# A transformer block's first stage: transposed x features on a second DMA queue, both value halves first, norm factor at eviction, memory features loaded transposed

## Chip, core and metric

One NeuronCore of a Trainium2 chip runs the whole program in one launch. The metric is the device time of one execution in microseconds (us); lower is better. TensorE is PE (its weight loads PEld), VectorE DVE, ScalarE ACT, GpSimd POOL, SyncE SP.

## The reference

A block of 256 positions with 1024 features: RMS norm and one input projection, spatial gating, forgetting attention, output projection, SwiGLU; then a second block with pooling, mLSTM, grouped attention, cross-attention to a memory of 256 rows and 16 experts. What the change touches:

```python
h = rmsnorm(x, mix_pre_g[l])
proj = h @ w_in[l]
u, v_s, q, k, v_a, g_a, g_b, f_logit = jnp.split(proj, IN_SPLITS, axis=-1)
...
merged = jax.nn.sigmoid(g_a) * y_a + jax.nn.sigmoid(g_b) * y_b
x = x + rmsnorm(merged @ w_out[l], mix_post_g[l])
...
kv = (mem @ wkv).reshape(b, mem.shape[1], 2, CA_HEADS, CA_HEAD_DIM)
```

Here `rmsnorm` is x * rsqrt(mean(x*x) + 1e-6) * g per position, `v_a` are the attention values, and `mem` is used without a norm.

## The kernel before

**Split weights.** A float32 matrix product is made of three products of float32r operands: high x low, low x high, high x high (`mm3`, lines 357 to 360; `wide`, lines 378 and 379, packs two of them into one matmul of 512 columns). So every operand is split into a high part, written by ACT, and a low part (value minus high), written by DVE. The dense weights arrive in 85 units of 1 MB, each in four pieces of 128x512. SP loads unit u into one of three buffers RAW (line 2300), waiting for the low parts of unit u-3. ACT's `high` (line 1048) and DVE's `low` (line 1575) write a piece into one of five pairs SPH and SPL. The constant `POOL_PIECES` gives some low parts to POOL instead (line 2194). Pieces are taken in strict order by number, unit 4u+q.

**Order of work.** Nothing is scheduled: each engine's program is written out by hand and runs in order, and engines wait on each other's counters. A wait or a DMA issue holds all that stands behind it on its engine.

**The start.** x arrives in three DMAs, position rows on partitions. ACT and DVE square it, POOL takes the power -0.5 (`power`, line 2185), DVE multiplies by that factor and by the gain (`first_norm`, line 1616; PE had spread the gain row over all partitions, line 418), PE transposes the result through PSUM (`turn_tile`, line 409), ACT and DVE write its high and low parts XTH and XTL (lines 1058 and 1580). Only then can the first product run: `rtile` (lines 389 to 400) for the first 512 value columns (units 0 and 1), tile t being 128 of the 256 positions. The second tile is transposed between (line 425). Then q and k of heads 0 to 3 (`wide`, units 2 to 5), the second 512 value columns (units 6 and 7, lines 466 to 470), q and k of heads 4 to 7, and so on. ACT copies finished values from PSUM to VA (`values_out`, line 1099). After its first sixteen weight pieces ACT issues nine DMAs for constants (lines 1085 to 1093).

**The output projection.** After the product for u (lines 517 to 523), PE transposes the memory rows (line 532, 16 transposes through all four PSUM banks), then runs `out_tile` (lines 535 to 545). It uses units 28 to 31, pieces 112 to 127; POOL writes the low parts of pieces 120 to 123. ACT and DVE then write the memory's high and low parts MEMH and MEML (lines 1208 and 1767), which `wblock` needs later (line 557).

**The end.** From about 500 us on SP fills the expert buffers RING (400 MB of expert weights), each fill waiting for an event of the dense part, and then streams all 16 experts.

Of the kernel before, what the change touches and what calls it, by code (L numbers as in the profile page):

```python
# [13 lines left out]
P = 128  # L14
T = 256
# [11 lines left out]
U_VA, U_Q, U_K = (0, 6), (2, 8), (4, 10)  # L27
# [6 lines left out]
POOL_PIECES = (120, 121, 122, 123, 279, 283, 287, 293, 294, 295, 298, 299, 302, 303, 306, 307, 310, 311, 322, 327, 331, 335)  # L34
# [53 lines left out]
def build(nc, ctx, io, out):  # L88
# [25 lines left out]
    PIOTA = place("PIOTA", [P, 4], F32, SMALL + 128)  # L114
    ONER = place("ONER", [16, P], F32R, low(14))
# [8 lines left out]

    QT = place("QT", [P, 8, T], F32, at(135))
# [21 lines left out]
    MEM = place("MEM", [P, 2, D], F32, at(185))  # L147
# [86 lines left out]
    GROW = place("GROW", [1, D], F32, at(201))  # L234
# [70 lines left out]
    rn = {n: small() for n in ss}  # L305
    fox_small = [[small(2) for _ in range(3)] for _ in range(8)]
# [40 lines left out]
    def tensor(e):  # L347
# [66 lines left out]
        for _ in range(7):  # L414
            e.matmul(PB[4][:, 0:P], WARM[:, :], WARM[:, :], start=True, stop=True)
        e.wait_ge(s_row, 16)
        for i in range(2):
            e.matmul(PB[6 + i][:, :], WARM[0:1, :], GROW[:, halves[i]], start=True, stop=True).then_inc(*mixd.up(("gain", i)))  # L418
        for _ in range(2):
            e.matmul(PB[4][:, 0:P], WARM[:, :], WARM[:, :], start=True, stop=True)  # L420
        e.wait_ge(s_id, 16)
# [8 lines left out]
        free = {0: vec.at(("xt_in", 1, 0)), 1: vec.at(("xt_in", 1, 1)), 2: act.at(("va", 0, 0)), 3: act.at(("va", 0, 1))}  # L430
# [63 lines left out]
        for h in range(2):  # L494
            for t in range(2):
                bank = 2 - 2 * h + t
                e.wait_ge(*free[bank])
                rtile(U_VS + 2 * h, bank, t, [("xt_in", t, j) for j in range(2)], ("vs", h, t))
                free[bank] = act.at(("vs", t, h))
# [26 lines left out]
        e.wait_ge(s_mem, 16)  # L526
        for t in range(2):
            for j in range(2):
                b = 2 * t + j
                e.wait_ge(*free[b])  # L530
                for k in range(4 * j, 4 * j + 4):
                    i = e.transpose(PB[b][:, (k % 4) * P:(k % 4 + 1) * P], MEM[:, t, k * P:(k + 1) * P], ident)
                i.then_inc(*turn.up(("mem", t, j)))

# [497 lines left out]
    def scalar(e):  # L1032
        done = [0]

        def high(n):

            for _ in range(n):
# [35 lines left out]
        e.dma_start(X[:, 0, 512:1024], io["x"][0:P, 512:1024]).then_inc(s_x[1], 16)  # L1073
        e.dma_start(GROW[:, :], io["mix_pre_g"].rearrange("(a n) -> a n", a=1)).then_inc(s_row, 16)
        squares_in(0, 0, "x0", (s_x[0], 16))
        high(2)
        for j in range(2):
            high_turned(0, j, j, XTH, turn.at(("in", 0, j)), "xt_in")
        high(2)
        pre_squares(1, "x1", [(s_x[2], 16)] * 2)  # L1080
        high(4)
        for j in range(2):
            high_turned(1, j, j, XTH, turn.at(("in", 1, j)), "xt_in")
        high(8)
# [60 lines left out]

        for half_ in range(2):
            for t in range(2):
                values_out(half_, t)
# [10 lines left out]
            if half_ == 0:  # L1159
                high(8)  # L1160
# [1388 lines left out]
```

## Time and profile before

| | |
|---|---|
| median of 3 runs | 1486.63 us (1486.63 to 1488.58) |
| the profiled execution | 1486.36 us, of which span 1484.6 us |
| PE busy | 1147.1 us (77%) |
| DVE, ACT, POOL busy | 468.4, 398.3, 74.1 us |
| DMA | 503.33 MB, mean 339 GB/s |

The profile is one execution. Its 40 slices show PE at nine tenths in the first 14 and at five to six tenths after; the DMA engines are at nine tenths from about the 16th on. The two stretches have to be read apart: in each it is asked what PE waits for.

### The profile page before, as it was taken

How to read it: one execution, taken by the hardware profiler on the slowest of the kernel's cores; microseconds unless marked ns; L12 is line 12 of the kernel's file. 1: busy time of each engine (PE TensorE's matmuls, PEld its weight loads, DVE VectorE, ACT ScalarE, POOL GpSimd, SP SyncE). 2: the span in 40 equal slices, each digit the busy share in tenths (PEclk: the TensorE clock that was granted, in tenths of full speed). 3: DMA queues.
4: the chain of work that ended last, by engine and by line, in shares of the span. 5: the costliest groups of instructions: out<-in, count | busy, mean ns of one | idle time of the engine just before them, and what ended most of it. 6: DMA issues, size and time to landing. Idle time of an engine off the chain costs nothing.

```text
span 1484.6 us, 19383 instructions
## 1 busy us (share of the span) xinstructions
PE 1147.1 (77%) x8336; PEld 754.3 (51%) x8336; DVE 468.4 (32%) x954; ACT 398.3 (27%) x890; POOL 74.1 (5%) x89
## 2 busy tenths in 40 slices
PE   9999999999999998995566466566665564565677
PEld 7888988888877875442322223223222232232234
DVE  6575777656788764110000000000000000000002
ACT  5665567555657642110000000000000000000002
POOL 0000020000035411000000000000000000000000
PEclk9999999999999998798778778787887787887789
DMA  8435546555553488999999999999999999999996
GB/s 313 171 138 203 198 172 223 208 207 199 199 187 114 149 347 343 397 436 434 433 437 426 433 433 435 424 442 430 430 437 426 438 430 433 433 426 440 423 424 288
DMA packets 29450, 503.33 MB, mean 339 GB/s; under 512 B 4275, under 2 KB 4915, under 8 KB 8245
## 3 DMA queue, kind: packets, MB, share of 16 engines
q1 hardware_dynamic: 25344, 493.43, 79.7%
q10 hardware_dynamic: 4020, 8.66, 1.6%
q8 instruction: 66, 1.08, 0.3%
q14 instruction: 20, 0.16, 0.0%
HBM read 501.03 MB, written 1.05 MB: 338 GB/s over the span
## 4 chain that ended last, share of the span: by engine, by line
issue 60%; PE 32%; DVE 5%; ACT 1%; POOL 1%; POOLq 0%; DVEq 0%; ACTq 0%
PE PB L378 9%; PE PB L358 5%; PE PB L359 5%; PE PB L360 5%; PE PB L379 4%; DVE SPL L1575 1%; DVE XN L1595 0%; PE PB L409 0%; POOL SP L2238 0%; PE PB L815 0%; PE PB L680 0%; PE PB L418 0%; PE PB L507 0%; PE PB L799 0%; PE PB L454 0%
## 5 line engine op out<-in xcount | busy, mean ns | idle before, releaser
L919 PE MATMUL PB<-RING,XS 128*32 128x512 f32 x2048 | 292.8, 720 | 177.0 <-DMA RING<-in_wgu_dram 176.7
L919 PEld LDWEIGHTS PB<-RING,XS 128*32 128x32 f32 x2048 | 68.4, 126 | 345.3 <-issue 249.8
L951 PE MATMUL PB<-RING,HHT 128*32 128x256 f32 x2048 | 150.9, 452 | 111.9 <-DMA RING<-in_wdn_dram 110.5
L1575 DVE TENSOR_TENSOR SPL<-RAW,SPH 128x512 fp32r<-128x512 f32 x318 | 207.0, 709 | 31.4 <-ACT SPH L1048 28.7
L378 PE MATMUL PB<-XT,SPH 128*128 128x512 f32 x544 | 194.1, 401 | 0.0
L1048 ACT ACTIVATE SPH<-RAW 128x512 fp32r<-128x512 f32 x340 | 186.8, 620 | 7.4 <-DMA RAW<-in_wst_dram 3.3
L951 PEld LDWEIGHTS PB<-RING,HHT 128*32 128x32 f32 x2048 | 75.3, 129 | 172.2 <-issue 141.7
L379 PE MATMUL PB<-XT,SPL 128*128 128x256 f32 x544 | 152.4, 280 | 0.0
L1506 ACT ACTIVATE SG<-PB 128x512 f32<-128x512 f32 x16 | 9.6, 597 | 506.1 <-PE PB L919 506.1
L2128 DVE SCALAR_TENSOR_TENSOR YL<-PB,COLS,YH 128x256 fp32r<-128x256 f32 x64 | 31.0, 484 | 279.0 <-ACT YH L1520 279.0
L378 PEld LDWEIGHTS PB<-XT,SPH 128*128 128x128 f32 x544 | 102.2, 188 | 24.6
L379 PEld LDWEIGHTS PB<-XT,SPL 128*128 128x128 f32 x544 | 102.7, 189 | 0.4
L1520 ACT ACTIVATE YH<-PB,COLS 128x256 fp32r<-128x256 f32 x64 | 30.3, 474 | 252.7 <-PE PB L951 252.7
L2118 DVE TENSOR_TENSOR SG<-SG,PB 128x512 f32<-128x512 f32 x16 | 11.0, 687 | 268.2 <-ACT SG L1506 268.2
L2113 DVE TENSOR_TENSOR XS<-PB,RG 128x256 f32<-128x256 f32 x15 | 6.4, 425 | 234.7 <-PE PB L905 234.7
L2185 POOL TENSOR_TENSOR SM<-SM,MH 128x1 f32<-128x1 f32 (+3 forms) x20 | 15.2, 762 | 1287.0 <-DVE SM L2170 886.7
L905 PEld LDWEIGHTS PB<-SEL,X 128*128 128x128 f32 x480 | 54.7, 192 | 12.1 <-issue 11.7
L905 PE MATMUL PB<-SEL,X 128*128 128x32 f32 x480 | 56.4, 277 | 0.3 <-DVE COLS L2132 0.3
L970 PEld LDWEIGHTS PB<-YL,GT 128*128 128x128 f32 x128 | 25.7, 201 | 41.8 <-issue 39.0
L358 PE MATMUL PB<-SPH,XT 128*128 128x512 f32 x112 | 44.9, 401 | 1.7 <-DVE XT L1580 1.7
L358 PE MATMUL PB<-XT,SPL 128*128 128x256 f32 x160 | 46.0, 287 | 0.0
L360 PE MATMUL PB<-XT,SPH 128*128 128x256 f32 x160 | 45.3, 283 | 0.0
(398 smaller groups left out, 1577.5 us busy)
## 6 DMA issues: line engine op xcount, KB each, us to landing
RAW<-in_wst_dram SPq DMA_DIRECT2D x84, 1024.0 KB, 4.9
RING<-in_wgu_dram SPq DMA_DIRECT2D x13, 2048.0 KB, 40.4
RING<-in_wgu_dram SPq DMA_DIRECT2D x4, 4096.0 KB, 22.3
RING<-in_wgu_dram SPq DMA_DIRECT2D x14, 1024.0 KB, 8.1
RING<-in_wdn_dram SPq DMA_DIRECT2D x6, 2048.0 KB, 13.4
RING<-in_wdn_dram SPq DMA_DIRECT2D x2, 4096.0 KB, 19.0
RING<-in_wdn_dram SPq DMA_DIRECT2D x3, 1024.0 KB, 41.0
RAW<-in_wst_dram SPq DMA_DIRECT2D x4, 256.0 KB, 5.6
```

The costliest lines, as they stand in the source:

```text
L358: e.matmul(out_, ll, rh, start=first, stop=False)
L359: e.matmul(out_, lh, rl, start=False, stop=False)
L360: return e.matmul(out_, lh, rh, start=False, stop=final)
L378: e.matmul(both, hv[:, k, c], XT[:, :, k, :], start=k == 0, stop=False)
L379: i = e.matmul(PB[bank][:, 0:T], lv[:, k, c], XTH[:, k, :], start=False, stop=k == KD - 1)
L905: i = e.matmul(PB[3][:, 32 * k:32 * k + 32], X[:, t, k * P:(k + 1) * P], SEL[:, t, 32 * x:32 * x + 32], start=t == 0, stop=t == 1)
L919: i = e.matmul(PB[b][32 * c:32 * c + 32, :], XS[x % 2][:, k, :], chunk_at(n)[:, 512 * c:512 * c + 512], start=k == 0, stop=k == KD - 1)
L951: w = e.matmul(PB[b][32 * j:32 * j + 32, 0:T], HHT[:, j, 32 * c:32 * c + 32], chunk_at(n)[:, T * (4 * (c % 2) + j):T * (4 * (c % 2) + j + ...
L1048: e.activation(h, src, ACT.Copy).then_inc(*hi.up())
L1520: e.activation(YH[m % 2][:, :], PB[3 - m % 2][:, 0:T], ACT.Copy, scale=COLS[:, 1, x:x + 1]).then_inc(*act.up(("y", x, m)))
L1575: e.tensor_tensor(l, src, h.bitcast(F32), ALU.subtract).then_inc(*lo.up())
L2128: e.scalar_tensor_tensor(out=YL[m % 2][:, :], in0=PB[3 - m % 2][:, 0:T], scalar=COLS[:, 1, x:x + 1], in1=YH[m % 2][:, :].bitcast(F32), op0 ...
```

## The change

- **x.** A transposed copy `xt` (feature on the partition, host layout) comes in four DMAs of 256 KB on ACT's queue, behind the gain as a column (`GCOL`, 4 KB). x itself, now needed only for the squares and the residual, moves on SP's queue behind the first three weight units. The ACT table is loaded by a small activation first. The identity moves from SP's to ACT's queue.
- **Rows without the norm factor.** For the first four feature blocks of tile 0 ACT and DVE multiply by the gain column and split in one step each (`high_first`, `low_first`). The other three quarters POOL multiplies by the gain (128x512 each), then ACT and DVE split them (`high_rows`, `low_rows`) into XRH and XRL. The fourth POOL multiply is for the first quarter itself.
- **Values first.** Units 0 to 3 are now the two value halves; each piece is used for both tiles. The norm factor is ACT's scale when it copies values out. PE's two products `norm_factors` (inside the second half) spread the factors over the partitions, DVE multiplies all of XR by them, ACT and DVE split that into XTH and XTL for all other projections. ACT's nine constant DMAs stand behind this split, and the two value evictions of half 0, the eight pieces of units 4 and 5, and the evictions of half 1 behind those.
- **Removed on PE.** 16 transposes and two gain products of the start, 16 transposes of the memory; 13 warming products in place of 7 + 2.
- **Memory.** It is loaded transposed; ACT and DVE split it from SBUF.
- **Pieces 120 to 123** move from POOL to DVE.

```diff
-U_VA, U_Q, U_K = (0, 6), (2, 8), (4, 10)
+U_VA, U_Q, U_K = (0, 2), (4, 8), (6, 10)
...
-POOL_PIECES = (120, 121, 122, 123, 279, 283,
+POOL_PIECES = (279, 283,
...
 def tensor(e):
...
-        rtile(U_VA[0], 2, 0, [("xt_in", 0, j) for j in range(2)], ("va", 0, 0), between=second_tile)
-        rtile(U_VA[0], 3, 1, [("xt_in", 1, j) for j in range(2)], ("va", 0, 1))
+        for half_ in range(2):
+            for j in range(2):
+                first_pairs = [(0, 0), (1, 0), (0, 1), (1, 1)]
+                for k, t in (first_pairs if half_ + j == 0 else [(k, t) for k in range(2) for t in range(2)]) + [(k, t) for k in (2, 3) for t in range(2)]:
...
+                    i = rk(U_VA[half_] + j, k, 4 * j + k, 2 - 2 * half_ + t, XRH, XRL, t, j + k == 0, j == 1 and k == 3)
...
+                    if (half_, j, k, t) == (1, 0, 1, 1):
+                        norm_factors()
+        free = {b: act.at(("va", int(b < 2), b % 2)) for b in range(4)}
...
-                for k in range(4 * j, 4 * j + 4):
-                    i = e.transpose(PB[b][:, (k % 4) * P:(k % 4 + 1) * P], MEM[:, t, k * P:(k + 1) * P], ident)
...
 def scalar(e):
+        e.dma_start(GCOL[:, :], io["mix_pre_g"]).then_inc(s_gcol, 16)
+        for j in range(2):
+            for t in range(2):
+                e.dma_start(XR[:, t, 4 * j:4 * j + 4, :], io["xt"][:, t, 4 * j:4 * j + 4, :]).then_inc(s_xt[2 * j + t], 16)
...
+        high_first(0)
+        high(1)
+        for k in range(1, 4):
+            high_first(k)
+        high(1)
+        high_rows(1, 0)
+        high(2)
+        high_rows(0, 1)
+        high_rows(1, 1)
+        high(4)
...
-            e.activation(VA[:, t, halves[half_]], PB[bank][:, :], ACT.Copy).then_inc(*act.up(("va", half_, t)))
+            e.activation(VA[:, t, halves[half_]], PB[bank][:, :], ACT.Copy, scale=rn[f"x{t}"]).then_inc(*act.up(("va", half_, t)))
...
+        for t in range(2):
+            values_out(0, t)
+        high(8)
+        for t in range(2):
+            values_out(1, t)
...
 def vector(e):
+            scaled_rows = XR[:, :, 4 * j:4 * j + 4, :].rearrange("p t k c -> p k t c")
+            factors = PB[6][:, 0:T].rearrange("p (t c) -> p t c", t=2).unsqueeze(1).to_broadcast([P, 4, 2, P])
+            e.tensor_tensor(scaled_rows, scaled_rows, factors, ALU.mult).then_inc(*vec.up(("n_in", j)))
...
 def gpsimd(e):
+        for t, j in ((1, 0), (0, 1), (1, 1), (0, 0)):
...
+            a = XR[:, t, 4 * j:4 * j + 4, :]
+            e.tensor_tensor(a, a, GCOL[:, 4 * j:4 * j + 4].unsqueeze(2).to_broadcast([P, 4, P]), ALU.mult).then_inc(*gps.up(("xg", t, j)))
...
-        low(120, 121, 122, 123)
...
 def sync(e):
+        for i in range(2):
+            c = slice(1024 * i, 1024 * i + 1024)
+            e.dma_start(RAW[1][:, c], io["wst"][1][:, c]).then_inc(s_next[i], 16)
+        e.dma_start(RAW[2][:, :], io["wst"][2]).then_inc(s_w[2], 16)
+        for t in range(2):
+            e.dma_start(X[:, t, :], io["x"][t * P:(t + 1) * P, :]).then_inc(s_x[t], 16)
```

**Place one: ACT, from the end of the first sixteen weight pieces to the values' evictions** (SPH is a piece's high part, the number its buffer; XT the normed input; VA the values; PB a PSUM bank). Before:

```order
L1048 ACTIVATE SPH3<-RAW0 128x512 [waits s_w0]
L1048 ACTIVATE SPH3<-RAW0 128x512 x3
L1085 DMA WFR<-in_wf_dram 128x1024
...
L1093 DMA PIOTA<-in_piota_dram 128x4
L1099 ACTIVATE VA<-PB2 128x512 [waits s_product]
L1099 ACTIVATE VA<-PB3 128x512 [waits s_product]
L1048 ACTIVATE SPH4<-RAW1 128x512 [waits s_w1]
```

Now:

```order
L1051 ACTIVATE SPH3<-RAW0 128x512 x3
L1109 ACTIVATE XT<-XR 128x1024 [waits s_formed] x2
L1111 DMA WFR<-in_wf_dram 128x1024
...
L1119 DMA PIOTA<-in_piota_dram 128x4
L1125 ACTIVATE VA<-PB2,SM 128x512 [waits s_product,s_pooled]
L1125 ACTIVATE VA<-PB3,SM 128x512 [waits s_product]
L1051 ACTIVATE SPH4<-RAW1 128x512 [waits s_w1]
L1051 ACTIVATE SPH4<-RAW1 128x512 x3
L1051 ACTIVATE SPH0<-RAW2 128x512 [waits s_product,s_w2]
L1051 ACTIVATE SPH0<-RAW2 128x512 x3
L1125 ACTIVATE VA<-PB0,SM 128x512 [waits s_product]
```

The split of the normed input, which waits for DVE (`s_formed`), now stands ahead of the nine DMAs, and the eviction that frees bank 0 behind eight more weight pieces. PE's first product of q writes bank 0.

**Place two: DVE, the start** (SPL is a piece's low part; XRL that of a row quarter). Before:

```order
L1616 SCALAR_TENSOR_TENSOR XN<-X,SM,PB6 128x512 [waits s_mixed,s_pooled]
L1616 SCALAR_TENSOR_TENSOR XN<-X,SM,PB7 128x512 [waits s_mixed]
L1575 TENSOR_TENSOR SPL0<-RAW0,SPH0 128x512 [waits s_high] x2
L1580 TENSOR_TENSOR XT<-PB0,XT 128x4x128 [waits s_activated]
L1580 TENSOR_TENSOR XT<-PB1,XT 128x4x128 [waits s_activated]
```

Now:

```order
L1649 SCALAR_TENSOR_TENSOR XRL<-XR,GCOL,XRH 128x128 [waits s_activated,s_xt0,s_gcol]
L1604 TENSOR_TENSOR SPL0<-RAW0,SPH0 128x512 [waits s_high]
L1649 SCALAR_TENSOR_TENSOR XRL<-XR,GCOL,XRH 128x128 [waits s_activated] x3
L1604 TENSOR_TENSOR SPL0<-RAW0,SPH0 128x512 [waits s_high]
L1641 TENSOR_TENSOR XRL<-XR,XRH 128x4x128 [waits s_activated]
L1604 TENSOR_TENSOR SPL0<-RAW0,SPH0 128x512 [waits s_high] x2
L1641 TENSOR_TENSOR XRL<-XR,XRH 128x4x128 [waits s_activated] x2
```

PE's second product (feature block 1, tile 0) waits for the second weight piece, behind three short rows; its first product for tile 1 waits for the first L1641. Each of the rows of now reads two operands from SBUF; of those of before L1580 and L1616 read one from PSUM.

**Place three: POOL, the start.** Before:

```order
L2196 MEMSET WARM 128x128
L2197 MEMSET MH 128x16
L2198 MEMSET ONER 16x128
L2185 ISA
L2185 TENSOR_TENSOR SM<-SM,MH 128x1 [waits s_formed,s_pooled]
```

Now, behind the same memsets:

```order
L2251 TENSOR_TENSOR XR<-XR,GCOL 128x512 [waits s_xt1,s_gcol]
L2251 TENSOR_TENSOR XR<-XR,GCOL 128x512 [waits s_xt2]
L2251 TENSOR_TENSOR XR<-XR,GCOL 128x512 [waits s_xt3]
L2251 TENSOR_TENSOR XR<-XR,GCOL 128x512 [waits s_xt0,s_formed]
L2230 TENSOR_TENSOR SM<-SM,MH 128x1 [waits s_formed,s_pooled]
```

The four multiplies by the gain stand ahead of the powers that give the norm factor; the fourth waits for DVE's short rows.

## Rows read from the trace of the kernel before

**Rows 1.** Busy time by stretch: each engine's us, granted clock, DMA share, GB/s.

```profile
40.00:200.00 160.00, 159.96 (x1022) 145.13 (x1022) 107.77 (x250) 97.23 (x220) 5.84 (x6) 1.00 0.47 173
600.00:1484.00 884.00, 565.87 (x5006) 259.73 (x4998) 60.43 (x131) 56.47 (x114) 0.82 (x1) 0.81 0.99 425
```

**Rows 2.** Timeline of PE at the start: start, us, instruction, idle before.

```profile
8.06 1.22 PE L420 MATMUL PB<-WARM 128*128 128x128 f32 x4
11.54 0.79 PE L358 MATMUL PB<-SPH,XT 128*128 128x512 f32 x1 [0.56 <-DVE XT L1580]
12.99 0.63 PE L358 MATMUL PB<-SPH,XT 128*128 128x512 f32 x1
13.42 0.63 PE L359 MATMUL PB<-SPL,XT 128*128 128x512 f32 x1
15.52 0.40 PE L358 MATMUL PB<-SPH,XT 128*128 128x512 f32 x1
25.07 0.39 PE L360 MATMUL PB<-SPH,XT 128*128 128x512 f32 x1
25.30 0.39 PE L378 MATMUL PB<-XT,SPH 128*128 128x512 f32 x1
```

**Rows 3.** DMA issues to 30 us: count, KB each, median us to landing.

```profile
RAW<-in_wst_dram SPq DMA_DIRECT2D x4, 256.0 KB, 5.6
X<-in_x_dram ACTq DMA_DIRECT2D x1, 256.0 KB, 3.4
```

**Rows 4.** The first six us, columns as in rows 1.

```profile
0.00:6.00 6.00, 4.94 (x16) 3.89 (x17) 0.86 (x3) 2.00 (x3) 1.14 (x8) 1.00 0.62 182
```

**Rows 5.** Timelines of POOL, of DVE beside it, and of DVE alone.

```profile
195.79 5.96 POOL L2194 TENSOR_TENSOR SPL<-RAW,SPH 128x512 fp32r<-128x512 f32 x4 [46.75 <-ACT SPH L1048]
198.81 1.78 DVE L1575 TENSOR_TENSOR SPL<-RAW,SPH 128x512 fp32r<-128x512 f32 x1
19.67 4.89 DVE L1575 TENSOR_TENSOR SPL<-RAW,SPH 128x512 fp32r<-128x512 f32 x8
```

**Rows 6.** POOL's and DVE's lines, durations ns min/median/max, then DVE and POOL groups.

```profile
L2194 POOL TENSOR_TENSOR SPL<-RAW,SPH x22: 1270/1594/1879, 195.8 to 537.9; 128x512 fp32r<-128x512 f32 x22
L2253 POOL TENSOR_TENSOR RWG<-RW,RG 128x128 f32<-128x128 f32 x1 | 0.9, 932 | 0.0
L1602 DVE TENSOR_TENSOR XN<-PB,G 128x512 f32<-128x512 f32 x8 | 5.2, 683 | 2.5 <-ACT JUNK L1067 2.5
L1786 DVE TENSOR_TENSOR FL<-FL,PB 128x256 f32<-128x256 f32 x22 | 9.3, 421 | 24.7 <-ACT FL L1240 24.7
```

**Rows 7.** Timeline of ACT and its issue queue (ACTq) before the first eviction; eight pieces elsewhere.

```profile
18.76 0.36 ACTq L1085 DMA_DIRECT2D WFR<-in_wf_dram  x1
22.82 0.48 ACTq L1093 DMA_DIRECT2D PIOTA<-in_piota_dram  x1
23.35 0.60 ACT L1099 ACTIVATE VA<-PB 128x512 f32<-128x512 f32 x1 [1.25 <-PE PB L360]
209.93 4.26 ACT L1048 ACTIVATE SPH<-RAW 128x512 fp32r<-128x512 f32 x8
```

**Rows 8.** PE after a wait in the expert stage, and that stretch by the us.

```profile
811.52 1.08 PE L919 MATMUL PB<-RING,XS 128*32 128x512 f32 x4 [5.32 <-DMA RING<-in_wgu_dram]
813.00:814.00 1.00, 1.00 (x8) 0.20 (x4) 0.00 (x0) 0.00 (x0) 0.00 (x0) 0.50 0.60 262
815.00:816.00 1.00, 1.00 (x16) 0.36 (x12) 0.00 (x0) 0.00 (x0) 0.00 (x0) 1.00 1.51 655
```

**Rows 9.** Timeline of PE, ACT and DVE around the memory's transposes.

```profile
192.60 2.17 PE L532 MATMUL PB<-CON,MEM 128*128 128x128 f32 x16
194.52 0.47 PE L358 MATMUL PB<-SPH,MTL 128*128 128x512 f32 x1
195.10 1.14 ACT L1048 ACTIVATE SPH<-RAW 128x512 fp32r<-128x512 f32 x2
195.22 0.42 DVE L1741 TENSOR_TENSOR MTL<-QT,MTH 128x256 fp32r<-128x256 f32 x1 [0.48 <-ACT MTH L1191]
```

More of the change, by code:

```diff
@@ L267, in build @@
     s_first = [sem(f"s_first{q}") for q in range(4)]
+    s_next = [sem(f"s_next{i}") for i in range(2)]
     s_w = [sem(f"s_w{i}") for i in range(NRAW)]
@@ L413, in tensor @@
         e.wait_ge(*gps.at("warm"))
-        for _ in range(7):
+        for _ in range(13):
             e.matmul(PB[4][:, 0:P], WARM[:, :], WARM[:, :], start=True, stop=True)
[L416 to L421, printed above, removed]
@@ L497, in tensor @@
                 e.wait_ge(*free[bank])
-                rtile(U_VS + 2 * h, bank, t, [("xt_in", t, j) for j in range(2)], ("vs", h, t))
+                rtile(U_VS + 2 * h, bank, t, [("xt_in", j) for j in range(2)], ("vs", h, t))
                 free[bank] = act.at(("vs", t, h))
@@ L1205, in scalar @@
         e.wait_ge(*vec.at(("gu", 7)))
-        for t in range(2):
-            for j in range(2):
-                high_turned(t, j, 2 * t + j, MEMH, turn.at(("mem", t, j)), "memt")
+        e.wait_ge(s_mem, 16)
+        for q in range(4):
+            e.activation(MEMH[:, 2 * q:2 * q + 2, :], MEM[:, 2 * q:2 * q + 2, :], ACT.Copy).then_inc(*act.up(("memt", q)))
         post_squares(0, "po0", "out")
@@ L1607, in postnorm @@
                 e.scalar_tensor_tensor(out=X[:, t, c], in0=XN[:, t, c], scalar=rn[name], in1=X[:, t, c], op0=ALU.mult, op1=ALU.add).then_inc(*vec.up((out_name, t, h)))
-        def first_norm(t, name):
-            e.wait_ge(*gps.at(("r", name)))
-            for h in range(2):
-                c = halves[h]
-                if t == 0:
-                    e.wait_ge(*mixd.at(("gain", h)))
-                e.scalar_tensor_tensor(out=XN[:, t, c], in0=X[:, t, c], scalar=rn[name], in1=PB[6 + h][:, :], op0=ALU.mult, op1=ALU.mult).then_inc(*vec.up(("n_in", t, h)))
@@ new lines, in vector, with low_first @@
+        e.wait_ge(s_gcol, 16)
+        e.wait_ge(s_xt[0], 16)
+        def low_first(k):
+            e.wait_ge(*act.at(("xr0", k)))
+            e.scalar_tensor_tensor(out=XRL[:, k, 0:P], in0=XR[:, 0, k, :], scalar=GCOL[:, k:k + 1], in1=XRH[:, k, 0:P].bitcast(F32),
+                                   op0=ALU.mult, op1=ALU.subtract).then_inc(*vec.up(("xr0", k)))
+        low_first(0)
+        low(1)
+        for k in range(1, 4):
+            low_first(k)
+        low(1)
+        low_rows(1, 0)
@@ new lines, in vector @@
+        low(2)
+        low_rows(0, 1)
+        low_rows(1, 1)
+        low(8)
+        for t in range(2):
+            e.wait_ge(s_x[t], 16)
+            e.tensor_tensor_reduce(XN[:, t, halves[1]], X[:, t, halves[1]], X[:, t, halves[1]], 1.0 / D, 0.0, ALU.mult, ALU.add, ss[f"x{t}"][1]).then_inc(*vec.up())
+        for t in range(2):
+            mean_square(f"x{t}", act.at((f"x{t}", 0)), vec.so_far())
+        low(4)
+        e.wait_ge(*gps.at(("xg", 0, 0)))
+        e.wait_ge(*mixd.at("r_in"))
@@ L1764, in vector @@
         low(8)
-        for t in range(2):
-            for j in range(2):
-                low_turned(t, j, 2 * t + j, MEMH, MEML, "memt")
+        for q in range(4):
+            e.wait_ge(*act.at(("memt", q)))
+            e.tensor_tensor(MEML[:, 2 * q:2 * q + 2, :], MEM[:, 2 * q:2 * q + 2, :], MEMH[:, 2 * q:2 * q + 2, :].bitcast(F32), ALU.subtract).then_inc(*vec.up(("memt", q)))
         postnorm(0, "po0", 1, 16, "res_mix")
```

130 lines of the change are left out of this document (69 added, 61 removed).

## The prediction

> **What bounds the kernel now.** I read the busy times by stretch first. From 40 to 200 us PE is busy for 159.96 of 160 us, and in the expert stage the DMA engines are at 0.99 of their time with 425 GB/s while PE waits [rows 1]. So the dense part ends when PE's list is done, and the expert stage, gated by events of the dense part, moves with it: a us gained or lost on PE at the start or around 195 us is a us of the whole time, and work on ACT, DVE or POOL counts only where PE waits for it. Second I read PE's timeline of the start. The first product starts at 11.54; its matmuls come 0.43 us apart (12.99, 13.42) until 15.52, and 0.23 apart later (25.07, 25.30); q starts at 25.30 [rows 2]. The granted clock reads 1.00 there too [rows 4], but 512 columns in 0.43 us are 1.2 GHz, and in 0.23 nearly 2.4. What stands before 11.54 is what the change attacks.
>
> **The yardstick.** The change puts both value halves ahead of q. Before, only one half lies ahead; the other's 48 matmuls come later, 48 x 0.228 = 10.9 us. So q of the changed kernel starts even with before at 25.3 + 10.9 = 36.2. Earlier is gain, later is loss, us for us.
>
> **Part 1: when the rows are there.** The first transposed quarter is second on ACT's queue, issued at about 1.3; an x half of the same size landed 3.4 us after its issue [rows 3], so it is there at about 4.7, and the first piece's split makes a first product possible at about 6.3. The second piece and the second quarter need four transfers, 1.05 MB, to have landed. In its first 6 us the kernel moved 6 x 182 = 1.09 MB [rows 4], so 6.1. Bound from above: the four first weight quarters took a median of 5.6 us to land [rows 3], 1 to 1.5 us later than this.
>
> **Part 2: POOL's multiplies hold DVE.** POOL has four new multiplies of 128x512. A POOL operation of that size takes 1.27 us at least [rows 6]. DVE's own pieces take 4.89 / 8 = 0.61 us apart alone, but one started at 198.81, while POOL did four, took 1.78 [rows 5], that is 0.68 and nearly a whole POOL operation. So I take turns: each multiply holds DVE for 1.27 us, then DVE does one row. DVE's short rows are an estimate: 0.68 at 512 and 0.42 at 256 columns [rows 6] give 0.29 at 128. From 6.2: three turns of 1.27 + 0.29 end at 10.9, the second piece is split at 11.5, the fourth multiply and the first rows of tile 1 end at 13.4. Only from there does PE run without gaps. By the Trainium skill, page SBUF — State Buffer, section Who interferes with whom, a tensor_tensor with two SBUF inputs and a GpSimd instruction that reads SBUF exclude each other for the whole instruction, which speaks against this placement; the 1.78 agrees, and by that rule the whole change costs the 4.3 us below. Read as mere slowing (DVE at 0.68/1.78 of its pace beside POOL), 4 x 1.27 = 5.1 us of POOL would cost DVE 3.1 instead of 5.1, and everything below would be 2 us less: +2.3. I take the turns, because four pieces beside POOL show the wait before an operation, not a longer one. Bounds: nothing (POOL ready while DVE is idle anyway), and 4 x 0.93 = 3.7 us for each multiply, if a broadcast multiply goes by the element like the 128x128 one [rows 6].
>
> **Part 3: to the norm factors.** PE's products for the factors stand behind 20 of 32 triples of matmuls. Two triples are done by 13.4, for tile 0 alone. The array stands at the lower level: before, it needed 11.54 to 15.52, 3.98 us, for three triples [rows 2]. So 13.4 + 4.0 + 15 x 3 x 0.228 = 27.6, and 28.0 with the two small products. DVE is not later: 14 pieces and two rows at 0.61, squares and small ones 1.8, from 13.4, is 25.0. X itself lands behind 3 MB of weights, and the powers follow DVE's squares at about 23; neither ends last.
>
> **Part 4: the queue on ACT.** Behind the factors: DVE multiplies twice 128x1024, an estimate by the same line as above 1.2 each, to 30.4. ACT's split waits for that, and in ACT's queue follow nine DMA issues. They cost 18.76 to 23.30, 4.5 us, and they hold ACT: its first eviction came at 23.35 after 1.25 us idle, put down to PE, which had long been done [rows 7]. Before, eight weight pieces queued ahead of them covered most of it; now nothing does. Then two evictions (1.1), eight pieces (4.26 [rows 7]), one eviction (0.6), which frees the bank of the first q product: 30.4 + 4.5 + 1.1 + 4.3 + 0.6 = 40.9. PE's values end at 28.0 + 36 x 0.228 = 36.2. So PE waits 4.7 us and q starts 4.7 us later than the 36.2 of before. The pieces of units 4 and 5 that q needs are behind the same queue and come 0.6 to 4 us earlier than the bank.
>
> **Part 5: the clock.** After a wait of 5.32 us the granted clock was 0.50 (1.2 GHz) from 813 to 814 and 1.00 (2.4 GHz) from 815 on: with the resumption at 811.5, some 3 us at half [rows 8]. I take the same for a wait of 4.7: 1.5 us of work. Bounds: nothing, and half of the 3.98 us at the lower level of the start [rows 2], 2.0.
>
> **Part 6: memory and output projection.** The 16 transposes go: 192.60 to 194.52, 1.9 us of PE [rows 9]. What covers: the first product needs no transpose; its eighth block needs the low part ending at 195.64, and comes at 192.6 + 7 x 0.68 = 197.4. Piece 120, now on DVE, is high at about 195.7 and low at 196.4 [rows 9], needed at 192.6 + 8 x 0.68 = 198.1; the next seven follow every 0.61 and are needed every 0.68. If DVE were 2 us late with them, the whole gain would be lost. ACT and DVE do the same number of splits for the memory as before.
>
> Nothing else: evictions with a scale are ACT rows as before; the start's 16 transposes and gain products lie inside parts 1 to 3; SP's fifth load waits for the same low parts.
>
> **Sum.** +4.7 + 1.5 - 1.9 = +4.3 us on the profiled execution's 1486.36, so **1490.7**. (The median of the runs is 0.3 above that execution.) What a measurement can tell from no change is 0.2%, 3 us.
>
> **Rivals.**
> - *POOL costs DVE little* (chance 0.25). Then the gap-free run starts at about 8.7, the factors are done at 8.7 + 4.0 + 10.2 + 0.4 = 23.3, q starts at 36.2, and the sum is 1.5 - 1.9: 1486.0. For it: before 6 us DVE has little, and multiplies that fit its waits are free. Against: 1.78 [rows 5].
> - *PE at the upper level from the start, and POOL mild: faster* (0.12). 13 warming products in place of 7. By the Trainium skill, page TensorE: Matmul & The Clock Gate, Part 1, sustained activity lifts the array's clock; in this trace the dummies did not: after them (8.06) the first real matmuls were still 0.43 apart [rows 2]. If it holds, 8.7 + 18 x 0.683 + 0.4 = 21.4 for the factors, q 1.8 before the yardstick, 1484.2; without the later fall of the clock 1482.7. It decides in favour when the factors' products are done before 23.7, 4.3 us ahead of my 28.0.
> - *POOL's broadcast multiplies are slow* (0.08): at 2 us each about 3 more, 1494; at 3.7, 1500.
>
> **Numbers.** Forecast 0.55, with 1488.7 to 1493 of its own. The range 1484 to 1495 leaves out most of the fast and slow rivals. Slower by over 0.2% (above 1489.6): 0.45 of the forecast, the slow rival and a little of the first, 0.55. Within 0.2%: 0.10 of the forecast and most of the first rival, 0.31. Faster: 0.14.
>
> **What would show it.** After: PE gap-free from about 13; POOL's four multiplies between 6 and 13 with DVE rows over 1 us long beside them; the factors' products near 28; ACT's nine issues from about 30 to 35 with ACT idle; a PE wait of 4 to 5 us ending near 41, with ACT's third eviction just before it, then matmuls at 0.43 us spacing. Wrong if that wait is absent, if DVE's early rows stay at 0.68, or if the output projection waits for pieces 120 to 127.

## The result, and the profile after

The changed kernel takes 1490.04 us (median of 13 runs, 1489.21 to 1492.61), the kernel before in the same measurement 1486.69 us (13 runs, 1484.79 to 1488.96). The ratio is 1.0026, its 95% interval 1.0019 to 1.0033: slower by 3.4 us. The profiled execution took 1490.07 us, 3.7 more than that of before. The forecast was 1490.7.

**A yardstick for the whole dense part.** Late in it PE waits for a normalised tile, in every kernel for the same 1 us. The start of the matmuls behind that wait is called M below. What happened earlier moves it, and what follows is the same program. Before, and after (timeline of PE: start, us, instruction, count, idle before and what ended it):

```profile
426.06 0.66 PE L409 MATMUL PB<-CON,XN 128*128 128x128 f32 x4 [1.02 <-DVE XN L1595]
```

```profile
430.31 0.66 PE L415 MATMUL PB<-CON,XN 128*128 128x128 f32 x4 [1.03 <-DVE XN L1624]
```

M went from 426.06 to 430.31, +4.25 us, beside a predicted sum of +4.3. From M to the end of the span it is 1058.54 us before and 1057.99 after; the 0.5 us between them is inside the scatter of that stretch (1057.1 to 1061.0 us over all profiles). From the first product of the output projection to M it is 231.5 us in every kernel but the one with pieces put back on POOL, so M follows the start us for us. The expert stage is what it was in [rows 1]:

```profile
600.00:1484.00 884.00, 575.10 (x5023) 262.96 (x5015) 60.58 (x132) 56.80 (x115) 0.81 (x1) 0.80 0.99 426
```

PE at the start, to be laid beside [rows 2]:

```profile
8.28 0.47 PE L364 MATMUL PB<-SPH,XRL 128*128 128x512 f32 x1 [2.53 <-DVE SPL L1604]
10.45 0.47 PE L364 MATMUL PB<-SPH,XRL 128*128 128x512 f32 x1 [1.24 <-DVE SPL L1604]
11.31 0.63 PE L364 MATMUL PB<-SPH,XRL 128*128 128x512 f32 x1
25.08 0.61 PE L428 MATMUL PB<-CON,SM 128*128 128x128 f32 x4
33.49 0.39 PE L366 MATMUL PB<-SPH,XRH 128*128 128x512 f32 x1
40.01 0.77 PE L384 MATMUL PB<-XT,SPH 128*128 128x512 f32 x1 [6.13 <-ACT VA L1125]
40.79 0.63 PE L384 MATMUL PB<-XT,SPH 128*128 128x512 f32 x1
45.26 0.39 PE L384 MATMUL PB<-XT,SPH 128*128 128x512 f32 x1
```

The first product comes 3.3 us earlier than before, but q starts at 40.01, 3.8 us behind the prediction's yardstick of 36.2, after a wait of 6.13 us for the eviction that frees its bank. The first eight steps of q then take 5.25 us (0.78 for the first, 0.64 for each of the others: 40.79, 41.43 and so on), and from 45.26 on a step takes 0.35. ACT in those microseconds, beside [rows 7]:

```profile
27.05 2.19 ACT L1109 ACTIVATE XT<-XR 128x1024 fp32r<-128x1024 f32 x2 [3.62 <-DVE XR L1673]
28.18 0.33 ACTq L1111 DMA_DIRECT2D WFR<-in_wf_dram  x1
33.19 0.45 ACTq L1119 DMA_DIRECT2D PIOTA<-in_piota_dram  x1
33.77 1.27 ACT L1125 ACTIVATE VA<-PB,SM 128x512 f32<-128x512 f32 x2 [4.53 <-PE PB L366]
34.92 4.26 ACT L1051 ACTIVATE SPH<-RAW 128x512 fp32r<-128x512 f32 x8
39.08 1.25 ACT L1125 ACTIVATE VA<-PB,SM 128x512 f32<-128x512 f32 x2
```

The nine issues run from 28.18 to 33.64. ACT is idle for 4.53 us, and the profile puts it down to PE, which had finished half 0 long before; that it waited for its own queue is what the first experiment tests. Behind that stand two evictions, eight pieces and the eviction that frees bank 0. The granted clock (columns as in [rows 1]; the seventh is the clock):

```profile
11.00:12.00 1.00, 1.00 (x4) 0.80 (x3) 1.00 (x1) 0.39 (x2) 0.84 (x1) 0.55 1.10 451
39.00:40.00 1.00, 0.00 (x0) 0.02 (x1) 1.00 (x1) 1.00 (x3) 0.64 (x1) 0.50 0.83 164
46.00:47.00 1.00, 1.00 (x7) 0.86 (x7) 0.91 (x2) 0.88 (x2) 0.00 (x0) 1.00 0.00 0
```

0.50 is the level of 1.2 GHz, 1.00 that of 2.4. It falls twice: at 11, after waits of 2.53 and 1.24 us (until 15), and during the wait for q. POOL and DVE at the start:

```profile
8.50 1.05 POOL L2251 TENSOR_TENSOR XR<-XR,GCOL 128x512 f32<-128x512 f32 x1 [7.32 <-DMA XR<-in_xt_dram]
12.74 2.59 POOL L2251 TENSOR_TENSOR XR<-XR,GCOL 128x512 f32<-128x512 f32 x2 [0.90 <-DMA XR<-in_xt_dram]
8.05 1.65 DVE L1649 SCALAR_TENSOR_TENSOR XRL<-XR,GCOL,XRH 128x128 fp32r<-128x128 f32 x3
12.91 2.97 DVE L1641 TENSOR_TENSOR XRL<-XR,XRH 128x512 fp32r<-128x512 f32 x2
```

POOL waited for its quarters, so its multiplies lie between 8.5 and 15.3, spread out; beside them two of DVE's rows are long (2.97 us together). At the memory, beside [rows 9], the last product of u is followed at once by the output projection:

```profile
198.72 0.28 PE L366 MATMUL PB<-XT,SPH 128*128 128x256 f32 x1
198.84 0.40 PE L364 MATMUL PB<-SPH,MTL 128*128 128x512 f32 x1
```

Read at three places the balance is: q +3.81 (40.01 for 36.2); at the end of u +6.24 (198.84 for 192.60), so 2.43 more from the half speed behind the wait; at the first product of the output projection +4.32 (198.84 for 194.52), so the transposes gave back 1.92.

### The profile page after: what moved, and what is told of

It reads as the page before. It is cut to its first block, busy times and chain, and to the rows that moved or that the text cites. A ratio compares the mean times of both kernels' runs of the same rounds, so it can differ in the third digit from the quotient of the medians.

```text
span 1488.3 us, 19356 instructions
## 1 busy us (share of the span) xinstructions
PE 1147.0 (77%) x8312; PEld 752.9 (51%) x8312; DVE 475.4 (32%) x963; ACT 401.0 (27%) x894; POOL 72.8 (5%) x89
## 3 DMA queue, kind: packets, MB, share of 16 engines
HBM read 502.08 MB, written 1.05 MB: 338 GB/s over the span
## 4 chain that ended last, share of the span: by engine, by line
issue 60%; PE 31%; DVE 5%; ACT 2%; ACTq 0%; DMA 0%; POOL 0%; POOLq 0%; DVEq 0%
PE PB L384 9%; PE PB L364 5%; PE PB L366 5%; PE PB L365 5%; PE PB L385 4%; DVE SPL L1604 1%; ACT SPH L1051 1%; DVE XN L1624 0%; DMA XR<-in_xt_dram 0%; PE PB L815 0%; PE PB L518 0%; ACT SP L1391 0%; PE PB L799 0%; PE PB L455 0%; PE PB L470 0%
## 5 line engine op out<-in xcount | busy, mean ns | idle before, releaser
L2230 POOL TENSOR_TENSOR SM<-SM,MH 128x1 f32<-128x1 f32 (+3 forms) x20 | 15.3, 765 | 1338.8 <-DVE SM L2215 886.3
L366 PE MATMUL PB<-XT,SPH 128*128 128x256 f32 x160 | 45.3, 283 | 0.0
L365 PE MATMUL PB<-XT,SPH 128*128 128x256 f32 x160 | 45.2, 283 | 0.0
## 6 DMA issues: line engine op xcount, KB each, us to landing
RING<-in_wdn_dram SPq DMA_DIRECT2D x6, 2048.0 KB, 13.4
```

The lines of the kernel that those rows point to most:

```text
L365: e.matmul(out_, lh, rl, start=False, stop=False)
L366: return e.matmul(out_, lh, rh, start=False, stop=final)
```

## The experiments

Each ran beside the kernel before on one chip, with five rounds of timing. The chips differ from set to set, but the kernel before took 1486.5 to 1486.8 us on all of them, so the medians can be laid side by side. **Theory A**: q is late by ACT's order, the nine issues and the bank; the clock's fall is a loss of its own; the memory part is a gain by itself. **Theory B**: q is late because POOL and DVE are slow at the start.

### Undoing ACT's order: issues, banks, both

The nine issues behind the evictions:

```diff
-        e.dma_start(WFR[:, :], io["wf"]).then_inc(s_wf, 16)
...
         for t in range(2):
             values_out(1, t)
+        e.dma_start(WFR[:, :], io["wf"]).then_inc(s_wf, 16)
...
```

> The changed kernel, with ACT's nine constant DMAs moved from behind the split of the normed input to behind the evictions of both value halves. Theory A (the nine issues hold ACT 5.5 us and with it the eviction that frees q's first bank): the two evictions of half 0 come at about 29.3 instead of 33.8, the eight pieces end at 34.7, q starts at about 35.4 instead of 40.0; the wait of PE shrinks from 6.1 to 1.5 us. That is 4.6 us, and 7.0 us if the clock then no longer falls (2.4 us at half speed). So 4.6 to 7.0 us under the changed kernel. Theory B (q waits for the normed input itself, that is for DVE and POOL at the start): q stays within 1 us of 40.0 and the time does not change.

Measured: 1485.18 us, ratio to before 0.9996 (0.9987 to 1.0004), 4.9 us under the changed kernel by the medians.

```profile
29.63 1.25 ACT L1116 ACTIVATE VA<-PB,SM 128x512 f32<-128x512 f32 x2
35.86 0.47 PE L384 MATMUL PB<-XT,SPH 128*128 128x512 f32 x1 [1.49 <-DVE SPL L1604]
```

The evictions came at 29.6, the wait shrank to 1.49, the clock stayed at 1.00 behind it, and M is 423.81, 6.5 less. Theory A, and in its numbers. B falls as the main cause.

The banks exchanged:

```diff
-                    i = rk(U_VA[half_] + j, k, 4 * j + k, 2 - 2 * half_ + t, XRH, XRL, t, j + k == 0, j == 1 and k == 3)
+                    i = rk(U_VA[half_] + j, k, 4 * j + k, 2 * half_ + t, XRH, XRL, t, j + k == 0, j == 1 and k == 3)
-        free = {b: act.at(("va", int(b < 2), b % 2)) for b in range(4)}
+        free = {b: act.at(("va", b // 2, b % 2)) for b in range(4)}
-            bank = t if half_ else 2 + t
+            bank = 2 * half_ + t
```

> The changed kernel, with the banks of the two value halves exchanged: half 0 writes banks 0 and 1, half 1 banks 2 and 3, so that q's first product needs the eviction of half 0 instead of that of half 1. The nine issues stay where they are. Theory A (bank 0 is what PE waits for): q then waits for the first piece of unit 4, which follows the two evictions at 33.8 to 34.9, high at 35.5 and low at 36.1: q at 36.1 instead of 40.0, a PE wait of 2.2 us; 3.9 us less, up to 6.3 if the clock does not fall. Theory B (normed input): no change.

Measured: 1486.64 us, 1.0004 (0.9995 to 1.0013), 3.4 under the changed kernel. The absolute times of the expectation missed, because in this execution the first quarter of x landed late: ACT waited 3.68 us for it.

```profile
8.61 0.40 ACT L1084 ACTIVATE XRH<-XR,GCOL 128x128 fp32r<-128x128 f32 x1 [3.68 <-DMA XR<-in_xt_dram]
11.10 0.76 PE L364 MATMUL PB<-SPH,XRL 128*128 128x512 f32 x1 [4.79 <-DVE SPL L1604]
39.73 0.47 PE L384 MATMUL PB<-XT,SPH 128*128 128x512 f32 x1 [1.81 <-DVE SPL L1604]
```

So the first product is 2.8 us later than in the changed kernel's profile and the last value product 4.0 (37.53 for 33.49), and still q starts 0.3 earlier, after a wait of 1.81 (2.2 expected) for the first piece and with no fall of the clock. M is 427.69, 2.6 less.

Both edits:

> Both edits of the two kernels beside this one: issues late and banks exchanged. Theory A: the first pieces of unit 4 are split at about 31 to 32, bank 0 is free at 30, the normed input's low parts end at 30.5, so PE goes from the last value product at 33.9 to q without a wait; 6.1 us of wait and 2.4 us of half speed go, 8.5 us under the changed kernel and some 5 under the kernel before. Theory B: no change. If the wait goes but the time falls by less than 7, the expert stage does not follow the dense part us for us.

Measured: 1484.16 us, 0.9984 (0.9974 to 0.9994): 2.4 under before, 5.9 under the changed kernel, less than the 8.5 expected.

```profile
34.38 0.39 PE L366 MATMUL PB<-SPH,XRH 128*128 128x512 f32 x1
34.61 0.39 PE L384 MATMUL PB<-XT,SPH 128*128 128x512 f32 x1
```

The wait is gone altogether. M is 422.49, 7.8 less, though the last value product came 0.9 later than in the changed kernel's profile (34.38 for 33.49): read at M, the 8.5 are there. That the medians show 5.9 may have two sources, neither tested by itself: landings differ from run to run, and from M to the end the span took 1057.1 to 1061.0 us over all profiles of this study, with no clear relation to M. So a difference of two medians is uncertain by a us and more, and M is the sharper reading.

### The memory part alone

The kernel before with the memory loaded transposed, its transposes removed and pieces 120 to 123 on DVE (the hunks of the change for `POOL_PIECES`, `MEM` and `memt`, and nothing else):

```diff
-POOL_PIECES = (120, 121, 122, 123, 279,
+POOL_PIECES = (279,
...
-                    i = e.transpose(PB[b][:, (k % 4) * P:(k % 4 + 1) * P], MEM[:, t, k * P:(k + 1) * P], ident)
...
+            e.activation(MEMH[:, 2 * q:2 * q + 2, :], MEM[:, 2 * q:2 * q + 2, :], ACT.Copy).then_inc(*act.up(("memt", q)))
```

> The kernel before with the last part of the change alone: memory loaded transposed, its 16 transposes removed, pieces 120 to 123 on DVE instead of POOL. Theory A: 1.9 us less than before, no PE wait in the output projection. Rival (the pieces or the memory's split come late on DVE, or the transposes only filled a wait for the first low part of the product's input): PE waits 0.6 to 2 us in the output projection and the time changes by less than 1 us.

Measured: 1484.61 us beside 1486.58, ratio 0.9990 (0.9980 to 0.9999), 2.0 us less.

```profile
26.03 0.39 PE L378 MATMUL PB<-XT,SPH 128*128 128x512 f32 x1
193.32 0.40 PE L358 MATMUL PB<-SPH,MTL 128*128 128x512 f32 x1
```

q began 0.73 us later than in [rows 2], the output projection 1.20 earlier than in [rows 9]: 1.93 in between, and PE waits nowhere in it. As expected. With that gain taken out, the rest of the change cost 4.25 + 1.92 = 6.2 us at M.

The pieces put back on POOL in the changed kernel:

```diff
-POOL_PIECES = (279,
+POOL_PIECES = (120, 121, 122, 123, 279,
...
+        low(120, 121, 122, 123)
```

> The changed kernel with the low parts of pieces 120 to 123 back on POOL. Theory A (DVE has time for them): no PE wait in the output projection with or without, and the time does not change (within 0.5 us); beside POOL some DVE rows last 1.8 us again. Rival (moving them to DVE gained or cost something): over 1 us either way, with a PE wait near 200 to 215 us.

Measured: 1494.28 us, 1.0045 (1.0031 to 1.0059), 4.2 over the changed kernel (2.7 over its control run below). Theory A missed here, and the rival holds:

```profile
203.23 5.93 POOL L2239 TENSOR_TENSOR SPL<-RAW,SPH 128x512 fp32r<-128x512 f32 x4 [46.74 <-ACT SPH L1051]
206.63 0.39 PE L366 MATMUL PB<-SPH,MTH 128*128 128x512 f32 x1
207.53 0.50 PE L364 MATMUL PB<-SPH,MTL 128*128 128x512 f32 x1 [0.50 <-POOL SPL L2239]
208.10 0.39 PE L366 MATMUL PB<-SPH,MTH 128*128 128x512 f32 x1
209.21 0.50 PE L364 MATMUL PB<-SPH,MTL 128*128 128x512 f32 x1 [0.73 <-POOL SPL L2239]
```

Without the transposes PE reaches pieces 120 to 123 sooner than POOL, at 1.48 us each, has them: two waits. The rows give them as 1.23 us of idle time, but read from start to start they cost 1.8: 0.90 from 206.63 to 207.53 and 1.11 from 208.10 to 209.21, and 0.33 and 0.34 from the first matmul behind each to the next, where matmuls otherwise come 0.23 apart. At M the kernel is 3.0 behind; q's own start, 41.22, is 1.2 of that, and the two waits are the rest.

### The clock, taken by itself

24 products of the warming tile between the last value product and q:

```diff
+        for _ in range(24):
+            e.matmul(PB[4][:, 0:P], WARM[:, :], WARM[:, :], start=True, stop=True)
+
         def fox_scores(h):
```

> The changed kernel with 24 matmuls of the warming tile on PE between the last value product and q, some 5.3 us of a wait of 6.1. Nothing that q waits for changes. Theory A (the fall of PE's clock after the wait is a loss of its own): q still starts near 40.0, but its matmuls come 0.34 us per pair at once instead of 0.64 up to 45.1; the time falls by 2.4 us. Rival (the clock falls there whatever PE does, or the loss is made up later): no change. Another rival (the matmuls hold up q): up to 1 us slower.

Measured: 1489.55 us, 1.0022 (1.0013 to 1.0031), only 0.5 under the changed kernel by medians.

```profile
36.38 5.52 PE L449 MATMUL PB<-WARM 128*128 128x128 f32 x48
41.80 0.50 PE L384 MATMUL PB<-XT,SPH 128*128 128x512 f32 x1
42.25 0.40 PE L384 MATMUL PB<-XT,SPH 128*128 128x512 f32 x1
```

q runs at 0.35 us a step at once. This execution started late (first product at 9.73), so q came 1.79 later than in the changed kernel, yet M is 429.78, 0.53 earlier: 2.3 us made up, next to 2.4 expected (next to the control run below it is 1.5, because there the clock cost less). The half speed is a loss of its own, shown at M, not in the medians.

More warming products at the start of the changed kernel:

```diff
-        for _ in range(13):
+        for _ in range(24):
             e.matmul(PB[4][:, 0:P], WARM[:, :], WARM[:, :], start=True, stop=True)
```

> The changed kernel with 24 warming products in place of 13, so that PE is busy until about 8.2 instead of 5.8. Theory A (the clock rises under the dummies and falls at 11 because PE then waited 2.5 us for its first and 1.2 us for its second product): the clock stays at the upper level, the matmuls from 11 to 14.6 come 0.23 instead of 0.43 us apart, the factors' products come 1.5 to 1.8 us earlier, and with them ACT's queue and q: 1.5 to 1.8 us less. Rival (the array must be busy with products for some us before the clock rises, dummies or not): no change, or 0.2 us slower.

Measured: 1491.09 us, 1.0028 (1.0016 to 1.0040): no gain.

```profile
1.06 8.56 PE L421 MATMUL PB<-WARM 128*128 128x128 f32 x48 [1.06 <-POOL MH L2242]
9.37 0.47 PE L364 MATMUL PB<-SPH,XRL 128*128 128x512 f32 x1
12.69 0.50 PE L364 MATMUL PB<-SPH,XRL 128*128 128x512 f32 x1 [1.69 <-DVE XRL L1641]
10.00:11.00 1.00, 1.00 (x5) 0.48 (x3) 0.00 (x0) 0.48 (x1) 0.48 (x1) 1.00 1.02 408
```

The mechanism is right and the forecast wrong: the clock stays at 1.00 all through the start, but 24 products last until 9.3 and held the first product up by a us, and then PE waits 1.69 us for rows that POOL and DVE have not made. A faster PE at the start finds nothing to do.

### POOL's multiplies

Left out, for the timing alone (the rows then lack the gain):

```diff
-        for t, j in ((1, 0), (0, 1), (1, 1), (0, 0)):
...
-            e.tensor_tensor(a, a, GCOL[:, 4 * j:4 * j + 4].unsqueeze(2).to_broadcast([P, 4, P]), ALU.mult).then_inc(*gps.up(("xg", t, j)))
```

> The changed kernel with POOL's four multiplies by the gain left out (so the gain is missing from all rows but the first four blocks of tile 0, and from the normed input). Theory of the prediction (POOL holds DVE for whole operations, and that delays PE): DVE's rows of 128x512 beside them fall from 1.0 to 1.5 us each to 0.6 to 0.7, the second product comes 0.6 us earlier, PE runs without gaps from about 9.9, the factors and q come 0.6 us earlier, 2.3 if the clock then does not fall at 11; 0.6 to 2.3 us less. Rival (DVE's delay is covered, because the quarters land late and PE runs at half speed anyway): DVE's rows shorten, the factors' products stay within 0.3 us, no change of the time.

Measured: 1490.28 us, 1.0018 (1.0009 to 1.0027), by medians no change.

```profile
8.21 0.87 DVE L1649 SCALAR_TENSOR_TENSOR XRL<-XR,GCOL,XRH 128x128 fp32r<-128x128 f32 x3
11.90 0.69 DVE L1641 TENSOR_TENSOR XRL<-XR,XRH 128x512 fp32r<-128x512 f32 x1
24.01 0.61 PE L428 MATMUL PB<-CON,SM 128*128 128x128 f32 x4
38.73 0.77 PE L384 MATMUL PB<-XT,SPH 128*128 128x512 f32 x1 [5.92 <-ACT VA L1125]
```

The three short rows take 0.87 us instead of 1.65, a row of 128x512 0.69 instead of 1.5. The factors come 1.07 earlier, q 1.28, M (428.44) 1.9. Next to the control below the factors come 2.4 earlier and q 1.9. So POOL cost one to two us at the start, and the wait for ACT stayed at 5.92. At q this lies inside the first expectation (0.6 to 2.3), while the median did not change, as the rival said; it is far from B.

Then rows split block by block with the gain as a scale, POOL's multiplies behind them, on top of late issues and exchanged banks:

```diff
+        def high_rows(t, j):
+            e.wait_ge(s_xt[2 * j + t], 16)
+            for k in range(4 * j, 4 * j + 4):
+                high_first(k, t)
...
+            e.wait_ge(*vec.at(("xr1", 7)))
             a = XR[:, t, 4 * j:4 * j + 4, :]
```

> The kernel with late issues and exchanged banks, and beside that the rows of all four quarters split as those of the first are, with the gain as a scale on ACT and DVE, block by block; POOL's four multiplies by the gain come behind the last of these rows. Theory (POOL holds DVE at the start, and what is late there is PE's second and third product): the short rows take 0.29 us each instead of 0.55, the second product comes 0.6 us earlier, the factors and q about 1 us earlier than with late issues and exchanged banks alone; 0.5 to 1.5 us less. Rival (ACT pays: 12 short rows of 0.32 us in place of three of 0.57, 2.2 us more on an engine that the weight pieces need too): nothing gained, or up to 1 us lost.

Measured: 1483.08 us, 0.9978 (0.9969 to 0.9987), 1.1 under both edits alone. The factors came at 25.19 instead of 25.97 and q at 34.19 instead of 34.61, less than half of what was expected at q:

```profile
14.58 5.92 POOL L2251 TENSOR_TENSOR XR<-XR,GCOL 128x512 f32<-128x512 f32 x4 [13.39 <-DVE XRL L1643]
14.57 8.29 DVE L1603 TENSOR_TENSOR SPL<-RAW,SPH 128x512 fp32r<-128x512 f32 x8 [0.17 <-ACT SPH L1049]
25.19 0.99 PE L428 MATMUL PB<-CON,SM 128*128 128x128 f32 x4 [1.05 <-POOL SM L2231]
```

The rest of the hold only moved. Four POOL operations stretched eight pieces from 4.9 us [rows 5] to 8.29, so DVE's squares, POOL's powers and the factors were late, and PE waited 1.05 us.

The same with `range(20)` warming products:

> The same with 20 warming products in place of 13: at 0.36 us each (24 took 8.56 us) they end at 8.2, just when the first product can start. Theory A (the clock stays at the upper level when PE has no wait of over a us): no half speed between 9 and 14, q 1 to 1.7 us earlier than without. Rival (pieces and rows come no faster, PE waits for them instead): q within 0.4 us, no change of the time.

Measured: 1483.42 us, 0.9976 (0.9967 to 0.9985). The clock stayed at 1.00, the third triple of products came at 10.30 instead of 11.12, and q at 34.13 instead of 34.19: the rival. The changed kernel itself once more:

> The changed kernel itself once more, beside the two above on the same chip. If its start varies with the landing of the first transfers from run to run, its first product will not be at 8.28 again but between 8.2 and 11.1, q between 40.0 and 42, the time 1489 to 1493; its ratio to before 1.002 to 1.004.

Measured: 1491.58 us, 1.0031 (1.0019 to 1.0042); first product 8.35, factors 26.43, q 40.63 after a wait of 5.40, M 430.09.

```profile
34.38 1.26 ACT L1125 ACTIVATE VA<-PB,SM 128x512 f32<-128x512 f32 x2 [3.80 <-issue]
40.63 0.77 PE L384 MATMUL PB<-XT,SPH 128*128 128x512 f32 x1 [5.40 <-ACT VA L1125]
43.96 0.39 PE L384 MATMUL PB<-XT,SPH 128*128 128x512 f32 x1
```

The first number of this start repeats, the next ones vary by up to 1.4 us. Two readings of the changed kernel's profile come out differently here. ACT's idle time is put down here to "issue", which means that ACT waited for nothing that the profile shows; so it is in five of the seven profiles with this order, and PE is named in two. And the clock was back at 43.96, 3.3 us after q began, not 5.2.

Last, on top of these rows and the 20 products, with the gain multiplied in the same operations as the norm factor, and no multiply on POOL:

```diff
-            e.tensor_tensor(scaled_rows, scaled_rows, factors, ALU.mult).then_inc(*vec.up(("n_in", j)))
+            for k in range(4 * j, 4 * j + 4):
+                i = e.scalar_tensor_tensor(out=XR[:, :, k, :], in0=XR[:, :, k, :], scalar=GCOL[:, k:k + 1], in1=factors, op0=ALU.mult, op1=ALU.mult)
+            i.then_inc(*vec.up(("n_in", j)))
```

> The kernel with short rows and 20 warming products, and POOL's four multiplies gone: DVE multiplies by the gain in the same operations that multiply by the norm factor (eight rows of 128x256 of about 0.42 us, 3.4 us, in place of two of 1.2, 2.35 us). All of the computation is there. Theory (POOL's multiplies, moved behind the rows, held DVE's eight pieces for 3.4 us, and with them the squares, the powers and the factors): DVE's eight pieces take 4.9 us again instead of 8.3, the factors' products come at about 23.5 instead of 25.1, q at about 32.4 instead of 34.2; 1.7 us less than with short rows alone, some 1481.5. Rival (q is then held by the later end of DVE's scaling, or by the pieces of unit 4): q between 33 and 34.2, 0 to 1 us less.

Measured: 1482.18 us beside 1486.51, ratio 0.9968 (0.9956 to 0.9980): 4.3 us under before, the fastest of the study.

```profile
14.61 4.91 DVE L1603 TENSOR_TENSOR SPL<-RAW,SPH 128x512 fp32r<-128x512 f32 x8 [0.17 <-ACT SPH L1049]
23.69 0.61 PE L428 MATMUL PB<-CON,SM 128*128 128x128 f32 x4
32.33 0.39 PE L384 MATMUL PB<-XT,SPH 128*128 128x512 f32 x1
```

The pieces take 4.91 again, the factors come at 23.69 and q at 32.33, without a wait: the numbers expected, to 0.2 us. Next to the rows by block alone, M is 1.9 us less (1.7 expected) and the median 0.9.

| kernel | q starts | M | median us | ratio to before |
|---|---|---|---|---|
| before | 25.30 (36.2 with both halves) | 426.06 | 1486.69 | 1 |
| changed | 40.01 | 430.31 | 1490.04 | 1.0026 |
| changed, once more | 40.63 | 430.09 | 1491.58 | 1.0031 |
| issues late | 35.86 | 423.81 | 1485.18 | 0.9996 |
| banks exchanged | 39.73 | 427.69 | 1486.64 | 1.0004 |
| both | 34.61 | 422.49 | 1484.16 | 0.9984 |
| both, rows by block | 34.19 | 422.07 | 1483.08 | 0.9978 |
| and nothing on POOL, 20 products | 32.33 | 420.21 | 1482.18 | 0.9968 |

## Why the prediction was right, and where its steps were not

- **Sum and sign.** +4.3 predicted, +4.25 found at M, and by nearly the same three terms: q 3.8 late (4.7), the clock 2.4 (1.5), the memory -1.9 (-1.9). Two terms were off by 0.9 in opposite directions, so the total is better than its parts. In the control the terms are 4.4, 1.5 and -1.9, nearer to those of the prediction, and M is 4.0 later than before: the kinds of loss repeat, their sizes vary by up to a us. That q came so near to the 40.9 of the text is in part luck: the rows were later than in part 1 and POOL's hold was shorter than in part 2, and the two offset.
- **Part 1, the first rows: late by 2 us.** 6.3 predicted, 8.28 found. The first quarter was not there at 4.7: ACT began on it at 6.49 (at 6.3 to 6.7 in nine of twelve profiles, at 7.9 in two and at 8.61 in one). The row of one X half [rows 3] was no measure for four quarters on one queue beside the weights on the other; why they came later was not tested.
- **Part 2, POOL holds DVE: the mechanism right, the cost too high.** Two rows beside POOL took 2.97 us; in the kernel without it a row took 0.69. But the four multiplies did not come in a row from 6.2: they waited for their quarters. PE had no long gap after 10.45, where 13.4 was forecast, and leaving POOL out gave q 1.3 us (1.9 next to the control), not the 4.7 that separated the forecast from its first rival. By the Trainium skill, page SBUF — State Buffer, section Who interferes with whom, a DVE instruction with two SBUF inputs and a GpSimd instruction that reads SBUF exclude each other. The trace agrees in kind: DVE took 8.29 against 4.91 us for the same eight pieces, so it lost 3.4 us beside four POOL operations that lasted 5.92.
- **Part 3, the factors: forecast 3 us too late** (28.0; found 25.08, and 26.43 in the control), since part 2 fed it.
- **Part 4, ACT's queue: right, and nearly in price.** The issues took 5.5 us in this profile, not 4.5, but 4.7 in the control. Starting 2.2 us earlier and costing 1 more, q came at 40.0 instead of 40.9. This queue was the cause: moving the nine issues alone took the wait from 6.13 (5.40 in the control) to 1.49. That the first rival's q at 36.2 was possible is refuted too: without POOL's multiplies q still came at 38.73.
- **Part 5, the clock: right in kind, its size not constant.** From the start of q to the first product of the output projection it is 156.4 to 156.5 us in the values-first kernels whose clock stays up there, and 158.83 here: 2.4 us were lost, where the text took 1.5 and at most 2.0. In the control it is 157.98, a loss of 1.5, and in the other three kernels with this wait 1.8 to 2.4. The text took its price from a wait of 5.32 in the expert stage, where the clock was back at most 3.5 us after PE resumed [rows 8]; here, from 40.01, it took 5.2 us, in the control 3.3. With 24 products in the wait the loss was gone (156.51).
- **Part 6, memory and output projection: right, -1.9**, in the changed kernel and alone. The move of four pieces to DVE, which the text costed at nothing, is a condition of it: with POOL, 1.8 us come back in two waits.
- **The rival on the clock.** The text said the warming products did not raise the clock. In the changed kernel they did: the first two triples (three matmuls each) ran at 0.23 to 0.31 us a matmul, and only after the waits did the clock fall. But 13 products leave that to chance: in the nine profiles with 13 the clock fell at some time from 8.0 to 11.1 us, and with late issues, for one, already the first triple ran at 0.42 to 0.47. By the Trainium skill, page TensorE: Matmul & The Clock Gate, Part 1, sustained activity lifts the array's clock; the traces agree, with the granted clock at 1.00 and matmuls 0.22 to 0.34 us apart from the first triple on under 20 and 24 products. What the rival made of it, 1484.2 us, did not follow: at that speed PE waits for rows instead.

## What to carry to other kernels

When a step is moved ahead of a block of DMA issues on a compute engine, price the whole block as idle time of that engine, and ask which buffer the next reader waits for: here a later place for nine issues and an exchange of PSUM banks moved M by 7.8 us, while the values-first order that they repaired is then worth 1.7 to 2.3 (422.49 against 424.78 with the memory part alone, or against 426.06 less 1.92). Moving an operation to an idle engine does not make it free: POOL's multiplies stretched DVE's rows in both places where they were tried, until another DVE operation did their work in passing. Read such a change at a fixed point late in the program; single medians were too coarse here for effects of 1 to 2 us.

## What was not expected of the hardware

- **The issues' price.** The same nine DMA issues took 4.5 us before and 5.5 after (0.33 to 0.99 us each), by the same queue, and 4.7 to 5.2 in the six other profiles with that order.
- **The clock after a wait.** A wait of 1.49 us in one kernel, of 1.81 in another and of 1.69 in a third left the granted clock at 1.00; waits of 2.53 and 1.24 close together, and one of 6.13, brought it to 0.50. How long it stays there after PE resumes does not go by the wait: 5.2 us behind one of 6.13 and behind one of 5.36 (pieces on POOL), 3.3 behind one of 5.40 (the control), at most 3.5 behind one of 5.32.
- **Two records that differ.** In the start of before the matmuls were 0.43 us apart while the granted clock read 1.00; in the changed kernel's start the two agree (0.43 at 0.50). We trust the spacing of the matmuls in the first microseconds.
- **The rest of the program varies.** From M to the end it took 1057.1 to 1061.0 us. In five of the seven profiles at 1059.6 and more, and in none of the others, the clock fell a second time between 488 and 504 us (with the memory part alone, 1060.9, from 488 to 494). Whether that makes these runs long was not tried and stays open.
